# Part of a gate projection moved ahead of the transposes of the attention weights, and ScalarE's copies of them moved ahead of its gate work

## The chip, the cores and the metric

One Trainium2 chip, one of its cores. The number that counts is the time of one execution of the kernel on the device, in microseconds (us); the median of several runs is taken. Engines are called by their short names: PE is TensorE (matmuls), DVE is VectorE, ACT is ScalarE, POOL is GpSimd, SP is SyncE, which only starts transfers here.

## What is computed

The kernel runs two small two-layer blocks over 256 tokens of width 1024, in f32: a recurrent layer, an attention layer, a mixing layer with a convolution, and two feed-forward layers. Only the attention layer is touched:

```python
q, g = jnp.split(h @ w_in, 2, axis=-1)     # 8 heads of 128
s = q @ k.T * sm_scale, causal             # per head, 256 x 256
o = softmax(s) @ v
y = (o * jax.nn.silu(g)) @ w_out
```

With 256 tokens there is one block of keys, so every token attends to itself and the tokens before it.

## The kernel before, in words

**Matmuls.** A weight matrix comes in slabs of 128 x 2048 f32 (1 MB). ACT copies a slab into a rounded high part (line 624, `stream`), DVE subtracts to get the low part (line 1067, shown as L1017, its helper), and PE multiplies three times for each tile: high by high, high by low, low by high (`product`, lines 1578 to 1580). So a gate output, which is one tile of 128 features by 256 tokens summed over 8 input tiles, is 24 matmuls (`gate`, line 1776). `fill(k)` on ACT and on DVE splits all slabs up to k + 3. The raw slabs lie in five buffers, and SP starts a transfer into one as soon as DVE has made the low part of the slab that was in it. Slab 12 + n feeds the gate outputs 2n and 2n + 1.

**Order.** Each engine has its own instruction list, written out by hand, and runs it strictly in order; semaphores tie them together. An output in PSUM goes to one of 8 banks by a fixed table (`outputs`, line 166), and `bank_free` (line 1572) makes PE wait until the bank's last content has been read. Along the way of this stage these are: the output of gate 2 in the bank of the scores of head 0, the transposed weights of head 3 in the bank of gate 0, gate 3 in that of gate 1, and in the second half the transposed weights of head 7 in the bank of gate 4, gate 7 in that of gate 5. The output projection's first two outputs take the banks of gate 6 and of the product of head 4.

**The attention stage** runs twice, for heads 0 to 3 and 4 to 7 (`for h in (0, 4)`):
- PE (lines 1785 to 1794): scores of four heads (L1752, L1753), gate h, gate h+1, the transposes of the weights of heads h and h+1 (`turn_weights`, L1763, three each), gate h+2, the products with the values for h and h+1 (`weighted`, L1772 and L1773), the transposes of h+2 and h+3, gate h+3, the products of h+2 and h+3. After the second half comes the output projection (`block_of("ao", ...)`).
- DVE (lines 1340 to 1354): per head scale and mask (shown as L1020), maxima, negation, inverse of the sum, and the scaling of the weights (L1312, L1313), staggered over the four heads; then a slab's low part, `output` (product times gate), `output_low`, another slab and so on.
- ACT (lines 812 to 824): the exponentials of four heads (L794, L795), the silu of gates h and h+1 (L716), the copies of the transposed weights of h and h+1 from PSUM to SBUF (`turned_weights`, two copies a head), a slab's high part (`fill`), silu of h+2, the high parts of outputs h and h+1 (`output_high`), the copies for h+2 and h+3, silu of h+3, a slab in the first half, and the high parts of h+2 and h+3.

Exp and Silu need different function tables; the load is an instruction of its own on ACT (ACT_TABLE_LOAD). Copies of ACT made through the helper `copy` all carry line 624, and all two-operand instructions of DVE made through `tt_` or `stt` carry 1017 or 1020, so these are told apart by tile and shape: `w<-raw` is a slab, `t<-pb` the turned weights, `r<-t` an output's high or low part. The tiles are f (scores' inputs, silu outputs), acc and s (weights), t (turned weights, outputs), r (high and low parts).

Of the kernel before, what the change touches and what calls it, by code (L numbers as in the profile page):

```python
# [6 lines left out]
P, T, D, KT = 128, 256, 1024, 8  # L7
# [317 lines left out]
def two_block_program(nc, w_d, vec_d, c_d, cst_d, dft_d, rcnt_d, row_d, x_d, out_d):  # L325
# [6 lines left out]
    with ctx:  # L332
        def sb(name, shape, dt=f32):
            return ctx.enter_context(nc.sbuf_tensor(name, shape, dt))

        def sem(name):
            return ctx.enter_context(nc.semaphore(name))
# [8 lines left out]
        R2 = sb("r2", [P, RT, 2, T], f32r)  # L346
# [40 lines left out]
        s_ps = sem("s_ps")  # L387
# [75 lines left out]
        def H(kt):  # L463
            return H0[:, kt, :]

        def out_of(*name):
            return PB[OUT.bank[name]][:, 0:T]

        def bank_of(*name):
            return PB[OUT.bank[name]]  # L470
# [20 lines left out]
        def hi_of(R, i):  # L491
            return R[:, i, 0, :]
# [4 lines left out]
        def ended(*name):  # L497
            return s_ps, OUT.count[name]
# [120 lines left out]
        def _(e):  # L619
# [3 lines left out]
            def copy(out, in_, **kw):  # L623
                return e.activation(out, in_, ACT.Copy, **kw)  # L624
# [14 lines left out]
            def fill(k):  # L639
                stream(MATS[min(k + LOOK, len(MATS) - 1)])  # L640
# [68 lines left out]
            for q in range(2):  # L709
                half = F0f[:, 4 * q:4 * q + 4, :]  # L710
# [3 lines left out]
            def silu_gate(kind, d, F, done):  # L714
                p.wait_ge(*ended(kind, d))
                e.activation(F[:, d, :], out_of(kind, d), ACT.Silu).then_inc(done, 1)  # L716
# [73 lines left out]
            def softmax(heads):  # L790
                for h in heads:
                    mx, s = st8[:, h, :], Sb[h % 4]
                    p.wait_ge(s_ng, h + 1)
                    e.activation(s[:, 0:128], s[:, 0:128], ACT.Exp, bias=mx[:, 2:3], accum_out=mx[:, 4:5])  # L794
                    e.activation(s[:, 128:384], s[:, 128:384], ACT.Exp, bias=mx[:, 3:4],  # L795
                                 accum_out=mx[:, 5:6]).then_inc(s_ex, 1)

            def turned_weights(*heads):
                for h in heads:
                    m, a, b = PB[OUT.bank["t", h]], tt[2 * (h % 2)], tt[2 * (h % 2) + 1]  # L800
                    p.wait_ge(*ended("t", h))
                    if h >= 2:
                        p.wait_ge(*ended("pv", h - 2))
                    copy(a[:, :], m[:, 0:256])
                    copy(b[:, 0:P], m[:, 256:384]).then_inc(s_pt, 1)

            def output_high(*heads):
                for h in heads:
                    p.wait_ge(s_ot, h + 1)
                    copy(hi_of(R1, h), tt[4 + h % 4][:, :]).then_inc(s_ohi, 1)  # L810

            for h in (0, 4):
                softmax(range(h, h + 4))
                silu_gate("ag", h, F3, s_ag)
                silu_gate("ag", h + 1, F3, s_ag)
                turned_weights(h, h + 1)
                fill(12 + h // 2)
                silu_gate("ag", h + 2, F3, s_ag)
                output_high(h, h + 1)
                turned_weights(h + 2, h + 3)  # L820
                silu_gate("ag", h + 3, F3, s_ag)
                if h == 0:
                    fill(13)
                output_high(h + 2, h + 3)
# [744 lines left out]
        def _(e):  # L1569
            p = Port(e)  # L1570

            def bank_free(*name):
                if OUT.prev[name] is not None:
                    p.wait_ge(*freed(OUT.prev[name]))

            def product(out, a_hi, a_lo, b_hi, b_lo, start, stop):

                e.matmul(out, a_hi, b_hi, start=start, stop=False)  # L1578
                e.matmul(out, a_hi, b_lo, start=False, stop=False)  # L1579
                return e.matmul(out, a_lo, b_hi, start=False, stop=stop)  # L1580

            def weights(k):
                p.wait_ge(s_lo, k + 1)

            def tile_of(k, half, o, R, r, out, start, stop, tok):
                w = W[(k + 2) % NSPL]
                if tok:
                    ts = slice(half * P, half * P + P)
                    return product(out, R[:, r, 0, ts], R[:, r, 1, ts], w[:, 0, o:o + 256], w[:, 1, o:o + 256],
                                   start, stop)  # L1590
                cs = slice(o + half * P, o + half * P + P)
                return product(out, w[:, 0, cs], w[:, 1, cs], R[:, r, 0, :], R[:, r, 1, :], start, stop)
# [43 lines left out]
            def spread(out, col):  # L1636

                return e.matmul(out, col.broadcast_to([P, P]), ident, start=True, stop=True)  # L1638

            def plain(out, slab, o, rhs, start, stop):  # L1640

                return e.matmul(out, slab[:, o:o + P], rhs, start=start, stop=stop)  # L1642
# [4 lines left out]
            for a in range(2):  # L1647
                done = e.matmul(bank_of("n", 0)[:, a:a + 1], tt[0][:, a * P:a * P + P], ones_sb[:, 0:1], start=True,
                                stop=True)
# [4 lines left out]
            for a in range(2):  # L1654
                done = spread(bank_of("nr", 0)[:, a * P:a * P + P], c0[:, a:a + 1])
            done.then_inc(s_ps, 1)

            for kt in range(KT):
# [3 lines left out]
                for d in range(8):  # L1662
                    if kt == 0:
                        bank_free("u", d)
                    done = plain(out_of("u", d), slab, d * P, H(kt), kt == 0, kt == KT - 1)
# [13 lines left out]
            for d in range(8):  # L1679
                for kind, name in (("ga", "rg_w_a"), ("gx", "rg_w_x")):  # L1680
# [3 lines left out]
                    for r in (d // 2 * 2, d // 2 * 2 + 1):  # L1684
                        p.wait_ge(s_conv, 6 * (r // 2) + 4 + r % 2 + 1)
                        done = plain(out_of(kind, d), slab, r * 256 + d % 2 * P, F1[:, r, :], r % 2 == 0, r % 2 == 1)
# [4 lines left out]
            for kt in range(KT):  # L1691
                p.wait_ge(s_yt, kt + 1)
                for d in range(4):
# [4 lines left out]
                    done = plain(out_of("y", d), slab, kt * 256 + d % 2 * P, tt[kt][:, :], kt == 0, kt == KT - 1)  # L1698
                    if kt == KT - 1:
                        done.then_inc(s_ps, 1)  # L1700
            for d in range(4, 8):
# [3 lines left out]
                for kt in range(KT):  # L1705
                    done = plain(out_of("y", d), slab, kt * 256 + d % 2 * P, tt[kt][:, :], kt == 0, kt == KT - 1)
# [18 lines left out]
            for kt in range(KT):  # L1725
                keys(kt, (0, 0, ("k", 0)), (0, 1, ("k", 1)), (1, 0, ("k", 2)), (1, 1, ("k", 3)))
                if kt == 3:
                    bank_free("n", 1)
                    p.wait_ge(s_na, 7)
                    for a in range(2):  # L1730
                        done = e.matmul(bank_of("n", 1)[:, a:a + 1], NA[0][:, a * P:a * P + P], ones_sb[:, 0:1],
                                        start=True, stop=True)
                    done.then_inc(s_ps, 1)
                if kt == 5:
                    bank_free("nr", 1)
                    p.wait_ge(s_rc1, 1)
                    for a in range(2):
                        done = spread(bank_of("nr", 1)[:, a * P:a * P + P], c1[:, a:a + 1])
# [7 lines left out]
            def scores(heads):  # L1746
                for h in heads:
                    bank, q, k = PB[OUT.bank["s", h]], F0f[:, h, :], F1[:, h, :]
                    bank_free("s", h)
                    p.wait_ge(s_q, h + 1)  # L1750
                    p.wait_ge(s_k, h + 1)
                    e.matmul(bank[:, 0:128], q[:, 0:128], k[:, 0:128], start=True, stop=True)  # L1752
                    e.matmul(bank[:, 128:384], q[:, 128:256], k, start=True, stop=True).then_inc(s_ps, 1)  # L1753

            def turn_weights(*heads):
                p.wait_ge(s_cst, 16)
                for h in heads:
                    m = PB[OUT.bank["t", h]]
                    bank_free("t", h)
                    p.wait_ge(s_p, h + 1)  # L1760
                    for j in range(3):
                        js = slice(j * P, j * P + P)
                        done = e.transpose(m[:, js], Sb[h % 4][:, js], ident)  # L1763
                    done.then_inc(s_ps, 1)
# [8 lines left out]
                    e.matmul(PB[OUT.bank["pv", h]][:, 128:256], Vt[:, 1, cs], b[:, 0:P], start=False,  # L1773
                             stop=True).then_inc(s_ps, 1)

            def gate(d):
                k = 12 + d // 2
                weights(k)
                bank_free("ag", d)
                p.wait_ge(s_hqlo, 8)  # L1780
                for kt in range(KT):
                    done = tile_of(k, d % 2, kt * 256, R2, kt, out_of("ag", d), kt == 0, kt == KT - 1, False)
                done.then_inc(s_ps, 1)

            for h in (0, 4):
                scores(range(h, h + 4))
                gate(h)
                gate(h + 1)
                turn_weights(h, h + 1)
                gate(h + 2)  # L1790
                weighted(h, h + 1)
                turn_weights(h + 2, h + 3)
                gate(h + 3)
                weighted(h + 2, h + 3)
# [38 lines left out]
            for h in range(4):  # L1833
                bank_free("f", h)
                out = out_of("f", h)
                for a in range(2):
                    p.wait_ge(s_ac, 2 * h + a + 1)
                    e.matmul(out, AC[:, h, a, 0:P], acc[0][:, a * T:a * T + T], start=a == 0, stop=False)
                    done = e.matmul(out, AC[:, h, a, P:256], acc[0][:, (2 + a) * T:(3 + a) * T], start=False,
                                    stop=a == 1)  # L1840
# [9 lines left out]
            for j in range(31):  # L1850
                p.wait_ge(s_dg, j + 1)
                done = e.matmul(out_of("cv", 3), dg[j % 8], G0[:, 3, j:j + T], start=j == 0, stop=j == 30)  # L1852
# [168 lines left out]
            for a in range(2):  # L2021
                for c in range(2):
# [3 lines left out]
                    for g in (2 * c, 2 * c + 1):  # L2026
                        p.wait_ge(s_pq, 4 + g + 1)
                        for b in range(2):
                            done = e.matmul(bank_of("p", a, c)[:, g % 2 * 256:g % 2 * 256 + 256],
                                            rc[:, b, g, a * P:a * P + P], Q[:, b, g, :], start=b == 0, stop=b == 1)  # L2030
# [94 lines left out]
```

## Time and profile before

| | |
|---|---|
| median of 3 runs | 742.0 us (741.99 to 742.11) |
| profiled execution | 742.27 us |
| its span | 740.5 us |
| granted PE clock | 0.999 of full speed |
| busy PE / DVE / ACT | 715.0 / 502.9 / 396.5 us |
| DMA | 156.65 MB, mean 212 GB/s |

The span is what the hardware profiler saw of one execution, from the first to the last instruction; the execution's own time is 1.77 us longer. Matmuls overlap: one of 256 columns has a duration of 0.28 us in the timeline and the next starts 0.12 us later. So the pace of PE is read from starts. A row's bracket gives the idle time before it and what ended it. The stage that is changed runs from 187 to 227 us.

### The profile page before, as it was taken

How to read it: one execution, taken by the hardware profiler on the slowest of the kernel's cores; microseconds unless marked ns; L12 is line 12 of the kernel's file. 1: busy time of each engine (PE TensorE's matmuls, PEld its weight loads, DVE VectorE, ACT ScalarE, POOL GpSimd, SP SyncE). 2: the span in 40 equal slices, each digit the busy share in tenths (PEclk: the TensorE clock that was granted, in tenths of full speed). 3: DMA queues.
4: the chain of work that ended last, by engine and by line, in shares of the span. 5: the costliest groups of instructions: out<-in, count | busy, mean ns of one | idle time of the engine just before them, and what ended most of it. 6: DMA issues, size and time to landing. Idle time of an engine off the chain costs nothing.

```text
span 740.5 us, 9710 instructions
## 1 busy us (share of the span) xinstructions
PE 715.0 (97%) x3902; PEld 625.0 (84%) x3902; DVE 502.9 (68%) x801; ACT 396.5 (54%) x620; POOL 2.4 (0%) x8
## 2 busy tenths in 40 slices
PE   2999999999999999999999999999999999999996
PEld 1888889999899999888888888888878888888885
DVE  4889996999876879976754454555576544555444
ACT  4156545883874776658734434443666344344423
POOL 0000000000000000000000000000000000000000
PEclk9999999999999999999999999999999999999999
DMA  8999994699835342433755545554336445545201
GB/s 336 419 422 415 421 385 163 250 393 340 316 118 216 116 170 71 182 111 150 271 183 183 208 177 177 207 185 171 114 114 227 171 173 208 187 173 201 81 0 58
DMA packets 23229, 156.65 MB, mean 212 GB/s; under 512 B 2576, under 2 KB 2832, under 8 KB 5264
## 3 DMA queue, kind: packets, MB, share of 16 engines
q1 hardware_dynamic: 22608, 153.41, 55.0%
q0 software_dynamic: 576, 2.62, 0.9%
q8 instruction: 31, 0.51, 0.3%
q14 instruction: 14, 0.11, 0.0%
HBM read 154.97 MB, written 1.05 MB: 211 GB/s over the span
## 4 chain that ended last, share of the span: by engine, by line
PE 86%; DVE 8%; ACT 4%; issue 1%; DMA 1%; SPq 0%; DVEq 0%
PE pb L1578 20%; PE pb L1580 20%; PE pb L1579 20%; PE pb L1642 13%; DVE w L1017 3%; DVE raw L1020 2%; PE pb L1852 2%; PE pb L1963 1%; PE pb L1719 1%; PE pb L1718 1%; PE pb L1720 1%; DMA x<-x_dram 1%; ACT w L624 1%; PE pb L1638 1%; PE pb L1885 1%
## 5 line engine op out<-in xcount | busy, mean ns | idle before, releaser
L1017 DVE TENSOR_TENSOR w<-raw,w 128x2048 fp32r<-128x2048 f32 x97 | 221.3, 2291 | 141.1 <-ACT w L624 141.1
L624 ACT ACTIVATE w<-raw 128x2048 fp32r<-128x2048 f32 x97 | 184.7, 1912 | 135.8 <-PE pb L1580 114.7
L1578 PE MATMUL pb<-w,r 128*128 128x512 f32 (+1 forms) x640 | 244.7, 382 | 0.7 <-DVE r L1020 0.3
L1580 PE MATMUL pb<-w,r 128*128 128x512 f32 (+1 forms) x640 | 241.1, 377 | 0.0
L1579 PE MATMUL pb<-w,r 128*128 128x512 f32 (+1 forms) x640 | 240.7, 376 | 0.0
L1578 PEld LDWEIGHTS pb<-w,r 128*128 128x128 f32 x640 | 120.5, 188 | 23.3 <-issue 2.1
L1580 PEld LDWEIGHTS pb<-w,r 128*128 128x128 f32 x640 | 120.4, 188 | 22.5
L1579 PEld LDWEIGHTS pb<-w,r 128*128 128x128 f32 x640 | 120.6, 188 | 21.0
L1578 PE MATMUL pb<-r,w 128*128 128x256 f32 x288 | 82.5, 287 | 0.4 <-DVE r L1017 0.4
L1579 PE MATMUL pb<-r,w 128*128 128x256 f32 x288 | 81.5, 283 | 0.0
L1580 PE MATMUL pb<-r,w 128*128 128x256 f32 x288 | 81.5, 283 | 0.0
L1020 DVE SCALAR_TENSOR_TENSOR raw<-raw,acc 128x1024 f32<-128x1024 f32 x64 | 75.1, 1220 | 4.1 <-DMA raw<-w_dram 4.1
L1642 PE MATMUL pb<-h,ow 128*128 128x256 f32 x256 | 58.5, 392 | 1.7 <-ACT h L686 1.7
L1642 PEld LDWEIGHTS pb<-h,ow 128*128 128x128 f32 x256 | 50.5, 198 | 9.4 <-issue 1.9
L1578 PEld LDWEIGHTS pb<-r,w 128*128 128x128 f32 x288 | 55.2, 192 | 0.6 <-issue 0.6
L1579 PEld LDWEIGHTS pb<-r,w 128*128 128x128 f32 x288 | 55.2, 192 | 0.1
L1580 PEld LDWEIGHTS pb<-r,w 128*128 128x128 f32 x288 | 55.2, 192 | 0.0
L959 ACT ACTIVATE t<-pb,rn 128x256 f32<-128x256 f32 x44 | 20.7, 476 | 59.6 <-PE pb L1580 59.6
L1020 DVE SCALAR_TENSOR_TENSOR f<-f,vec 128x256 f32<-128x256 f32 x114 | 46.6, 480 | 0.2
L1020 DVE SCALAR_TENSOR_TENSOR t<-pb,rn,t 128x256 f32<-128x256 f32 x44 | 21.1, 483 | 22.8 <-ACT t L959 22.8
L1642 PE MATMUL pb<-t,ow 128*128 128x256 f32 x128 | 27.8, 379 | 0.0
L1642 PEld LDWEIGHTS pb<-t,ow 128*128 128x128 f32 x128 | 24.3, 190 | 3.3
(203 smaller groups left out, 657.2 us busy)
## 6 DMA issues: line engine op xcount, KB each, us to landing
raw<-w_dram SPq DMA_DIRECT2D x129, 1024.0 KB, 4.9
ow<-w_dram SPq DMA_DIRECT2D x8, 1024.0 KB, 14.2
ow<-w_dram SPq DMA_DIRECT2D x8, 512.0 KB, 17.0
oh<-w_dram SPq DMA_DIRECT2D x2, 1024.0 KB, 23.1
x<-x_dram SPq DMA_DIRECT2D x2, 512.0 KB, 6.1
f<-rc_dram POOLq DMA_DIRECT2D x1, 1024.0 KB, 5.1
acc<-row_dram POOLq DMA_DIRECT2D x2, 512.0 KB, 6.8
out_dram<-f SPq DMA_DIRECT2D x4, 256.0 KB, 2.3
```

What stands on the lines that cost most here:

```text
L624: return e.activation(out, in_, ACT.Copy, **kw)
L959: e.activation(tt[(at_ - 1) % 4][:, :], bank_of("gu", layer, i, a)[:, 0:T], ACT.Silu, scale=rn[:, 2 * layer, a:a + 1]).then_inc(s_sgt, 1)
L1017: return e.tensor_tensor(out, a, b, op)
L1020: return e.scalar_tensor_tensor(out, a, s, b, op0, op1, **kw)
L1578: e.matmul(out, a_hi, b_hi, start=start, stop=False)
L1579: e.matmul(out, a_hi, b_lo, start=False, stop=False)
L1580: return e.matmul(out, a_lo, b_hi, start=False, stop=stop)
L1638: return e.matmul(out, col.broadcast_to([P, P]), ident, start=True, stop=True)
L1642: return e.matmul(out, slab[:, o:o + P], rhs, start=start, stop=stop)
L1718: e.matmul(with_shift, w[:, 0, o:o + P], raw_key(kt), start=kt == 0, stop=False)
L1719: e.matmul(with_shift, w[:, 1, o:o + P], raw_key(kt), start=False, stop=False)
L1852: done = e.matmul(out_of("cv", 3), dg[j % 8], G0[:, 3, j:j + T], start=j == 0, stop=j == 30)
```

## The change

On PE, the first four of the eight input tiles of gate h+2 (12 matmuls) stand ahead of the transposes of heads h and h+1, and the last four where the whole gate stood; the bank is waited for ahead of the first part, and the semaphore raised at the end of the last. On ACT, `turned_weights(h, h + 1)` comes right after the exponentials, ahead of two silus, and `turned_weights(h + 2, h + 3)` ahead of `output_high(h, h + 1)`. DVE, SP and POOL keep their lists, and the bank table stays.

```diff
@@ scalar
             for h in (0, 4):
                 softmax(range(h, h + 4))
+                turned_weights(h, h + 1)
                 silu_gate("ag", h, F3, s_ag)
                 silu_gate("ag", h + 1, F3, s_ag)
-                turned_weights(h, h + 1)
                 fill(12 + h // 2)
                 silu_gate("ag", h + 2, F3, s_ag)
+                turned_weights(h + 2, h + 3)
                 output_high(h, h + 1)
-                turned_weights(h + 2, h + 3)
                 silu_gate("ag", h + 3, F3, s_ag)
@@ tensor
-            def gate(d):
-                k = 12 + d // 2
+            def gate(d, kts=range(KT)):
+                k, half = 12 + d // 2, d % 2
                 weights(k)
-                bank_free("ag", d)
+                if kts[0] == 0:
+                    bank_free("ag", d)
                 p.wait_ge(s_hqlo, 8)
-                for kt in range(KT):
-                    done = tile_of(k, d % 2, kt * 256, R2, kt, out_of("ag", d), kt == 0, kt == KT - 1, False)
-                done.then_inc(s_ps, 1)
+                for kt in kts:
+                    done = tile_of(k, half, kt * 256, R2, kt, out_of("ag", d), kt == 0, kt == KT - 1, False)
+                if kts[-1] == KT - 1:
+                    done.then_inc(s_ps, 1)
 
             for h in (0, 4):
                 scores(range(h, h + 4))
                 gate(h)
                 gate(h + 1)
+                gate(h + 2, range(0, 4))
                 turn_weights(h, h + 1)
-                gate(h + 2)
+                gate(h + 2, range(4, 8))
                 weighted(h, h + 1)
```

## Rows read from the trace of the kernel before

**Rows 1.** The page, section 1: busy time, share of the span, instructions

```profile
PE 715.0 (97%) x3902; PEld 625.0 (84%) x3902; DVE 502.9 (68%) x801; ACT 396.5 (54%) x620; POOL 2.4 (0%) x8
```

**Rows 2.** Waits of PE, whole span: us in total, times, longest

```profile
PE pb L1772 <- ACT t L624: 1.8, 2, 0.9
...
PE pb L1885 <- DVE x L1017: 0.9, 2, 0.7
```

**Rows 3.** PE's timeline, heads 0 to 3: start, duration, instruction, idle before

```profile
195.24 0.28 PE L1580 MATMUL pb<-r,w 128*128 128x256 f32 x1
195.75 0.52 PE L1763 MATMUL pb<-cst,acc 128*128 128x128 f32 x3 [0.23 <-DVE acc L1313]
197.03 0.52 PE L1763 MATMUL pb<-cst,acc 128*128 128x128 f32 x3 [0.77 <-DVE acc L1313]
197.31 0.36 PE L1578 MATMUL pb<-r,w 128*128 128x256 f32 x1
...
201.24 0.67 PE L1772 MATMUL pb<-t,f 128*128 128x256 f32 x2 [0.82 <-ACT t L624]
...
203.19 0.36 PE L1578 MATMUL pb<-r,w 128*128 128x256 f32 x1
...
206.15 0.60 PE L1772 MATMUL pb<-t,f 128*128 128x256 f32 x2
```

**Rows 4.** PE's timeline, heads 4 to 7

```profile
209.90 0.47 PE L1578 MATMUL pb<-r,w 128*128 128x256 f32 x1
...
215.84 0.82 PE L1763 MATMUL pb<-cst,acc 128*128 128x128 f32 x6
216.41 0.36 PE L1578 MATMUL pb<-r,w 128*128 128x256 f32 x1
...
219.59 0.67 PE L1772 MATMUL pb<-t,f 128*128 128x256 f32 x2
...
221.54 0.36 PE L1578 MATMUL pb<-r,w 128*128 128x256 f32 x1
...
225.61 0.70 PE L1772 MATMUL pb<-t,f 128*128 128x256 f32 x2 [0.95 <-ACT t L624]
...
226.94 0.36 PE L1578 MATMUL pb<-r,w 128*128 128x256 f32 x1
```

**Rows 5.** ScalarE's timeline, 198 to 225 us

```profile
198.69 1.28 ACT L716 ACT_TABLE_LOAD   x1
199.99 0.66 ACT L716 ACTIVATE f<-pb 128x256 f32<-128x256 f32 x2
200.53 1.01 ACT L624 ACTIVATE t<-pb 128x256 f32<-128x256 f32 x4
201.38 1.95 ACT L624 ACTIVATE w<-raw 128x2048 fp32r<-128x2048 f32 x1
...
203.44 0.77 ACT L624 ACTIVATE r<-t 128x256 fp32r<-128x256 f32 x2
...
217.05 1.28 ACT L716 ACT_TABLE_LOAD   x1
...
224.37 0.75 ACT L624 ACTIVATE r<-t 128x256 fp32r<-128x256 f32 x2 [2.41 <-DVE t L1017]
```

**Rows 6.** VectorE's timeline, 203 to 226 us

```profile
203.94 0.76 DVE L1017 TENSOR_TENSOR r<-t,r 128x256 fp32r<-128x256 f32 x2 [0.70 <-ACT r L624]
204.62 2.29 DVE L1017 TENSOR_TENSOR w<-raw,w 128x2048 fp32r<-128x2048 f32 x1
...
209.55 1.01 DVE L1020 SCALAR_TENSOR_TENSOR acc<-pb,cst 128x384 f32<-128x384 f32 x2
...
223.92 0.75 DVE L1017 TENSOR_TENSOR t<-pb,f 128x256 f32<-128x256 f32 x2
224.82 0.76 DVE L1017 TENSOR_TENSOR r<-t,r 128x256 fp32r<-128x256 f32 x2 [0.15 <-ACT r L624]
```

**Rows 7.** ScalarE's timeline, 40 to 46 us

```profile
44.44 0.39 ACT L624 ACTIVATE f<-pb 128x256 f32<-128x256 f32 x1 [0.82 <-PE pb L1642]
```

## The prediction

> **What bounds the kernel now.** The page's busy shares come first: PE is busy 97% of a 740.5 us span [rows 1], so only time in which PE stands still, or a slower PE, is worth anything. The view of PE's waits over the whole span comes second: outside the first stages one group stands out, L1772, the products of attention weights and values, which waited for ScalarE's copies, 1.8 us in two places [rows 2]. The idle times there go by modelled matmul ends, so I priced the stalls from starts in the timeline. Two paces are needed. A whole gate output, 24 matmuls, takes 206.15 - 203.19 = 2.96 us [rows 3], 0.12 each, so half of one is 1.48. Six transposes take 216.41 - 215.84 = 0.57, three 0.29 [rows 4].
>
> Five places where PE stands still between 195 and 227 us:
> - First four heads: gate(1) ends at 195.24 + 0.12 = 195.36, the turn of head 0 starts at 195.75 (0.39 lost).
> - It is through by 196.04; head 1's turn starts at 197.03, released by DVE's scaled weights (0.99 lost).
> - gate(2) runs 197.31 + 2.96 = 200.27; weighted(0) starts at 201.24 (0.97 lost), waiting for ScalarE's copy [rows 3]. ScalarE was in its chain: the table load at 198.69 right behind the exponentials, two silus at 199.99, the copies at 200.53 [rows 5].
> - Second four heads: gate(6) ends at 216.41 + 2.96 = 219.37, weighted(4) starts at 219.59 (0.22 lost). The turns of heads 4 and 5 don't wait.
> - gate(7) ends at 221.54 + 2.96 = 224.50, weighted(6) starts at 225.61 (1.11 lost) [rows 4]. The copies it wants stand on ScalarE behind two high parts, which waited 2.41 us for DVE [rows 5].
>
> Together 3.68 us. That is all this stage can give.
>
> **The change part by part, first half (heads 0 to 3).** Nothing is added or removed: the same matmuls, copies, silus and one table load per half in another order. No DMA moves; the slab copies keep their place among ScalarE's items, save that output_high now follows two turned_weights.
>
> PE puts 12 matmuls of gate(2) ahead of the turns: 195.36 + 1.48 = 196.84. They need slab 13 (gate(2) and gate(3) share it; its low part is well ahead of the softmax on DVE) and the bank of scores 0, which DVE has read by then. Turn 0 has been free to run since 195.75, so it takes 196.84 to 197.13; turn 1's release at 197.03 is past, so it ends at 197.41, 0.10 behind the old 197.31. The other half ends at 197.41 + 1.48 = 198.89. The half gate thus covers both first waits.
>
> ScalarE starts the copies where the table load stood, 198.69. Four copies take a slot of 201.38 - 200.53 = 0.85; from the first copy to weighted(0) it is 201.24 - 200.53 = 0.71 [rows 3, 5]. So weighted(0) starts at 199.40 and 0.51 of waiting is left. Both weighted take (203.19 - 201.24) - 0.57 = 1.38, to 200.78. Next late: head 3's turn writes the bank that silu(0) frees, and the silus are now behind the copies. Load at 199.54, silu at + 1.30 = 200.84 (the 1.30 is 199.99 - 198.69); one silu takes 0.39 (a pair lasts 0.66 and its slot is 0.54, so the second starts 0.27 behind the first), a signal 0.13 (0.71, less the 0.58 that two copies last: 1.01 for four, less half of their slot). Turn 3 is released at 201.36. Turn 2 fills 200.78 to 201.07; 0.29 is waited, and turn 3 ends at 201.65. gate(3) wants the bank of gate(1), freed at 201.11 + 0.39 + 0.13 = 201.63: no wait. gate(3) starts at 201.65, not 203.19: **1.54 us ahead**. It ends at 204.61.
>
> ScalarE: the four items ahead of the slab copy at 201.38 only swap places, so that copy and silu(2) keep their times and ScalarE is free at 203.44 as before [rows 5]. turned_weights(2,3) now stands there: head 2's weights reach PE at 203.44 + 0.71 = 204.15, before gate(3) ends. weighted(2,3) and four scores take 209.90 - 206.15 = 3.75 [rows 3, 4], so gate(4) starts at 208.36, not 209.90.
>
> The price lies on DVE. output_high(0,1) starts 0.85 later, at 204.29, so DVE's output_low starts at 204.79 instead of 203.94, and the slab subtraction queued behind it at 205.47 instead of 204.62 [rows 6], to 207.76 by its 2.29. Then output(2,3), high, low: undisturbed this takes 224.82 + 0.76 - 223.92 = 1.66, to 209.42. The softmax of heads 4 to 7 began at 209.55; before, output_high(2,3) waited for a slab copy on ScalarE, which now starts earlier because silu(3) does. So the delay is hidden and softmax gains 0.13.
>
> **Second half.** gate(4), gate(5): 208.36 + 5.94 (215.84 - 209.90) = 214.30; half of gate(6) to 215.78, turns (ready before) to 216.35, other half to 217.83. ScalarE leaves the exponentials at 217.05 - 0.13 = 216.92; weights reach PE at 217.63: weighted(4) doesn't wait and ends at 219.21. Load at 217.77, silu(4) at 219.07, turn 7's bank at 219.59; turn 6 ends at 219.50, 0.09 is waited, gate(7) starts at 219.88, not 221.54, and ends at 222.84. ScalarE's slab copy starts at 219.61; copy and silu take 203.44 - 201.38 = 2.06, so turned_weights(6,7) starts at 221.67 and head 6's weights are there at 222.38: the 1.11 us wait is gone, since the copies are now ahead of the high parts that wait for DVE. weighted(6,7) takes 226.94 - 225.61 = 1.33, so the output projection starts at **224.17, not 226.94: 2.77 us**. Its second bank is freed by DVE's output(4), the first of a pair that takes 0.75, at about 223.79 + 0.42 + 0.13 = 224.34, wanted three matmuls after the first, 224.17 + 0.37 = 224.54: close, but in time. As a check, stalls left are 0.51 + 0.29 + 0.09 = 0.89, with 3.68 before: 2.79.
>
> **Does it reach the end?** Behind 227 us PE's longest wait is the 0.7 us of L1885 [rows 2], DMA is far from full, and transfers start when a slab has been split, so all moves with PE. I carry 2.77 on, rounded to 2.8. The profiled execution took 742.27 (its span and 1.77 around it), 0.27 over the median of 742.0. 742.27 - 2.8 = 739.5 by the profile, 739.2 against the median.
>
> **A rule against the sum.** By the rows the silu follows 1.30 us after its load is issued, and the load directly follows the exponentials. The Trainium skill (ScalarE: Activation LUTs, What ACT_TABLE_LOAD costs) gives 1283 ns and a drain of about 1380 ns for every switch. The trace agrees with the first figure and shows no drain. What that would make of the time is rival E.
>
> **Rivals.** (A) The copies bring a table load of their own, since they now stand behind Exp. Then two switches of 1.30 each follow the exponentials. First half: weighted(0) at 200.70, turn 3 at 202.66, gate(3) at 202.95 (0.24 ahead), DVE's softmax one load later (about 210.7). Second half: exponentials end near 218.2, weighted(4) at 220.2, gate(7) at 222.5, projection at 226.75, 0.19 ahead: 741.8, no change. Against it: the copy at 44.44 ran behind the Exp of line 690, and what ended its idle time was PE, with no load between [rows 7]. The Trainium skill says the same (ScalarE: Activation LUTs, Table sets: the hidden batching unit): copy is in every set.
>
> (B) DVE's queue eats part of the gain. output_low(0,1), the slab subtraction, output(2,3) and softmax(4) stand behind output_high(0,1). If softmax starts 1.3 us late (210.7), all of ScalarE's times of the second half move with it: gate(7) starts 1.3 later than forecast and half the gain stays: 740.5. For it: the wait chain is real and its slack in the second half is nil once turn 7 waits for silu(4). Against: the 0.85 is known and absorbed.
>
> (C) Slower: the same queue, from the point at which softmax(4) starts over 2.8 us later than forecast, past 212.2. That takes more than one slab subtraction (2.29) of further delay, for instance two in a row (4.58): 4.58 - 2.8 = 1.8 slower, 743.8. Nothing in the rows adds a second one.
>
> (D) The turns are not what PE waits for once the half gate is there, but the half gate costs as much: re-entering the open bank of gate(2) is not seen in the trace. Bounds: nothing (same number of changes between kinds of matmul), or 0.3 us a half (near the 0.39 lost at the first turn, the largest step between kinds that the rows show). I take nothing; upper end 0.6, 739.8.
>
> (E) The silu's table switch, now between the copies and the banks that PE wants, takes longer than 1.30. Each extra us delays the release of turn 3, then softmax(4) with ScalarE's chain, and in the second half turn 7 once more: two us at the projection for each. At 2.77 / 2 = 1.4 extra the gain is gone: 742.0. Against it: the one switch whose follower had nothing else to wait for took 1.30 [rows 5]. The drain that the Trainium skill states in the section above is that case.
>
> **Numbers.** Forecast 0.85 (with D's cost inside), B 0.07, A 0.03, E 0.02, C 0.03. Downward, all five stalls gone would be 3.7: 738.3. The range goes from 738.3 to 740.5, which takes in D and B. A measurement tells 0.2%, 1.5 us, from no change: faster is below 740.5. The forecast and about half of B fall there: 0.88; the other half of B, A and E are the same: 0.09; slower 0.03.
>
> **What the changed profile should show.** PE: twelve matmuls at 195.4 to 196.8, turns with no idle before them, weighted(0) at about 199.4, gate(3) at 201.65 after 0.3 of waiting, scores of heads 4 to 7 about 1.5 earlier, the projection at 224.2. ScalarE: copies at 198.7 and the silu's load at 199.5, and no load ahead of the copies. DVE: slab subtraction at 205.5, softmax(4) at 209.4. It would be wrong if weighted(0) waits past 200, if softmax(4) starts after 210, or if the 2.8 us that PE is ahead at 224 are given back further on.

## The result and the profile after

The changed kernel took 739.29 us, the median of 6 runs (738.29 to 739.67), against 742.0 for the kernel before (740.69 to 742.52): a ratio of 0.9966 with a 95% interval of 0.9955 to 0.9976, 2.7 us faster. In two later sets on other occasions it was 0.9958 (0.9944 to 0.9972) and 0.9952 (0.9939 to 0.9964). The forecast was 739.2. The profiled execution took 739.67, its span 737.9.

The waits of PE over the whole span (total, times, longest; answers to [rows 2]):

```profile
PE pb L1888 <- DVE x L1017: 0.9, 2, 0.7
...
PE pb L1578 <- ACT f L624: 0.4, 1, 0.4
...
PE pb L1772 <- ACT t L624: 0.3, 1, 0.3
PE pb L1763 <- ACT f L716: 0.2, 1, 0.2
```

The wait for the copies has gone from 1.8 to 0.3 us. The small wait at L1763 is the one that the prediction named: turn 3, held by a silu (ACT f L716). PE's timeline through the stage (start, duration, instruction; answers to [rows 3, 4]):

```profile
189.90 0.35 PE L1578 MATMUL pb<-r,w 128*128 128x256 f32 x1 [0.36 <-ACT f L624]
...
197.16 0.92 PE L1763 MATMUL pb<-cst,acc 128*128 128x128 f32 x6
197.83 0.36 PE L1578 MATMUL pb<-r,w 128*128 128x256 f32 x1
...
199.77 0.67 PE L1772 MATMUL pb<-t,f 128*128 128x256 f32 x2 [0.26 <-ACT t L624]
...
201.82 0.55 PE L1763 MATMUL pb<-cst,s 128*128 128x128 f32 x3 [0.17 <-ACT f L716]
202.12 0.36 PE L1578 MATMUL pb<-r,w 128*128 128x256 f32 x1
```

```profile
216.20 0.82 PE L1763 MATMUL pb<-cst,acc 128*128 128x128 f32 x6
216.78 0.36 PE L1578 MATMUL pb<-r,w 128*128 128x256 f32 x1
...
218.28 0.60 PE L1772 MATMUL pb<-t,f 128*128 128x256 f32 x2
...
223.13 0.60 PE L1772 MATMUL pb<-t,f 128*128 128x256 f32 x2
...
224.36 0.36 PE L1578 MATMUL pb<-r,w 128*128 128x256 f32 x1
```

This execution reached gate(0) at 189.90, 0.48 later than the profiled one of before, after a wait of 0.36 that lies outside the change. Its row names ScalarE's copies of two earlier outputs (f), the first of which empties the bank that gate(0) writes; they stood behind the copy of a slab that had landed late:

```profile
187.57 1.91 ACT L624 ACTIVATE w<-raw 128x2048 fp32r<-128x2048 f32 x1 [0.57 <-DMA raw<-w_dram]
...
189.39 0.64 ACT L624 ACTIVATE f<-pb 128x256 f32<-128x256 f32 x2
```

So positions are compared with gate(0): the turns of heads 0 and 1 have no idle time before them, where there were two waits; weighted(0) has 0.26 instead of 0.82; the last weighted, at 223.13, has none. From gate(0) to the output projection PE took 224.36 - 189.90 = 34.46 us; before it was 226.94 - 189.42 = 37.52.

ScalarE behind the exponentials (answers to [rows 5]):

```profile
199.11 0.96 ACT L624 ACTIVATE t<-pb 128x256 f32<-128x256 f32 x4
200.09 1.28 ACT L716 ACT_TABLE_LOAD   x1
201.38 0.66 ACT L716 ACTIVATE f<-pb 128x256 f32<-128x256 f32 x2
...
203.99 1.02 ACT L624 ACTIVATE t<-pb 128x256 f32<-128x256 f32 x4
204.83 0.77 ACT L624 ACTIVATE r<-t 128x256 fp32r<-128x256 f32 x2
```

The copies run right behind the exponentials with no table load ahead of them, the second pair (203.99) is ahead of the high parts (204.83), and the silus 1.29 us after their load begins. VectorE (answers to [rows 6]):

```profile
205.33 0.76 DVE L1017 TENSOR_TENSOR r<-t,r 128x256 fp32r<-128x256 f32 x2 [2.48 <-ACT r L624]
206.01 2.29 DVE L1017 TENSOR_TENSOR w<-raw,w 128x2048 fp32r<-128x2048 f32 x1
...
209.79 1.01 DVE L1020 SCALAR_TENSOR_TENSOR acc<-pb,cst 128x384 f32<-128x384 f32 x2
```

Output_low came late, as forecast, after 2.48 us of waiting, and the slab behind it at 206.01, 16.11 behind gate(0) where it was 15.20 (204.62 [rows 6] - 189.42), but softmax(4) starts at 209.79, which is 19.89 behind gate(0), against 20.13 before (209.55 - 189.42). In the two later traces of the changed kernel it is 19.86 and 19.84.

### The profile page after: what moved, and what is told of

Its sections match the earlier page's. It is cut to its first block, busy times and chain, and to the rows that moved or that the text cites. A ratio compares the mean times of both kernels' runs of the same rounds, so it can differ in the third digit from the quotient of the medians.

```text
span 737.9 us, 9710 instructions
## 1 busy us (share of the span) xinstructions
PE 714.1 (97%) x3902; PEld 624.4 (85%) x3902; DVE 502.4 (68%) x801; ACT 396.3 (54%) x620; POOL 2.4 (0%) x8
## 4 chain that ended last, share of the span: by engine, by line
PE 88%; DVE 6%; ACT 3%; DMA 2%; issue 1%; SPq 0%; DVEq 0%
PE pb L1578 21%; PE pb L1580 21%; PE pb L1579 21%; PE pb L1642 13%; DVE w L1017 2%; PE pb L1855 2%; PE pb L1966 1%; DVE raw L1020 1%; DMA raw<-w_dram 1%; PE pb L1719 1%; PE pb L1718 1%; PE pb L1720 1%; DMA x<-x_dram 1%; PE pb L1888 1%; PE pb L1638 1%
```

## The experiments

All times are medians, with the kernel before run beside them on the same chip; the ratio is worked out from the single executions, so it differs a little from that of the two medians. A time of one execution carries what happened ahead of the stage, so for each trace I also give PE's time from the first matmul of gate(0) to the first of the output projection ("stage"), and within it up to gate(4) ("first half"). They repeat well: the changed kernel gave 34.46, 34.42 and 34.41.

| kernel | time | ratio to before (95%) | stage | first half | second half |
|---|---|---|---|---|---|
| before | 741.5 to 742.0 | 1 | 37.52 | 20.48 | 17.04 |
| changed (after) | 739.29 | 0.9966 (0.9955 to 0.9976) | 34.46 | 18.92 | 15.54 |
| e1, half gate alone | 742.70 | 1.0013 (1.0005 to 1.0022) | 39.15 | 22.10 | 17.05 |
| e2, ScalarE's order alone | 739.46 | 0.9973 (0.9965 to 0.9981) | 34.99 | 19.43 | 15.56 |
| e3, first copies alone | 740.33 | 0.9987 (0.9978 to 0.9995) | 36.45 | 19.41 | 17.04 |
| e4, second copies alone | 740.71 | 0.9985 (0.9976 to 0.9994) | 36.31 | 20.47 | 15.84 |
| after2 | 738.46 | 0.9958 (0.9944 to 0.9972) | 34.42 | 18.89 | 15.53 |
| e5, extra table switch | 741.42 | 1.0000 (0.9992 to 1.0009) | 37.43 | 20.38 | 17.05 |
| e6, half gate and filler | 741.82 | 1.0004 (0.9995 to 1.0013) | 37.47 | 20.41 | 17.06 |
| b3, banks, turn, DVE | 737.27 | 0.9942 (0.9928 to 0.9957) | 33.84 | 18.30 | 15.54 |
| after3 | 738.03 | 0.9952 (0.9939 to 0.9964) | 34.41 | 18.88 | 15.53 |
| b1, banks | 738.53 | 0.9959 (0.9946 to 0.9971) | 34.11 | 18.58 | 15.53 |
| b2, banks and turn | 738.62 | 0.9958 (0.9945 to 0.9972) | 34.13 | 18.57 | 15.56 |
| b3_again | 737.57 | 0.9946 (0.9933 to 0.9958) | 33.85 | 18.31 | 15.54 |

**The parts of the change.** e1 keeps the diff's PE part and puts ScalarE's list back; e2 is the reverse. e3 and e4 move one pair of copies each, with the old PE order:

```diff
 e3
                 softmax(range(h, h + 4))
+                turned_weights(h, h + 1)
                 silu_gate("ag", h, F3, s_ag)
                 silu_gate("ag", h + 1, F3, s_ag)
-                turned_weights(h, h + 1)
 e4
+                turned_weights(h + 2, h + 3)
                 output_high(h, h + 1)
-                turned_weights(h + 2, h + 3)
```

Expected of e1: 

> PE's half of the change alone, ScalarE in its old order. Theory L (a covered wait only moves to the next thing that is late, ScalarE's chain of exponentials, table load, silus, copies): PE is done with gate 2 at 198.9 instead of 200.3 and waits 2.3 us for the copies at weighted(0), which starts at 201.24 as before; the second half has no wait at its turns to cover. No change: 742.0, within 0.3. Rival R (the two waits at the turns, 0.39 + 0.99, are gained outright): 740.6.

Expected of e2: 

> ScalarE's half of the change alone, PE in its old order. Theory L: copies reach PE at 199.4, gate 2 ends at 200.27, so weighted(0) starts then: 0.97 ahead; second half: weighted(4) without its 0.22, weighted(6) without its 1.11. Sum 2.3, time 739.7; the whole change is then only 0.5 better than this part. Rival R (each half of the change removes its own waits): 742.0 less 0.97 + 0.22 + 1.11 is the same 2.3 here, but with the half gate alone at 1.4 the two would have to add to 3.7, which the whole change (2.7) does not show.

Expected of e3: 

> Only turned_weights(h, h+1) moved ahead of the two silus; output_high stays ahead of turned_weights(h+2, h+3), PE old. Theory L: first half 0.97 ahead; in the second half the 0.22 at weighted(4) goes, but the copies for weighted(6) still stand behind the high parts that wait for DVE's slab and output(4), so that wait grows to about 1.4. Sum about 0.9, time 741.1. Rival: that wait stays at 1.11 and 1.2 are gained, 740.8; the trace tells these apart by the idle time ahead of the last weighted.

Expected of e4: 

> Only turned_weights(h+2, h+3) moved ahead of output_high(h, h+1), PE old. Theory L: nothing in the first half (weighted(2) doesn't wait), output_low 0.6 to 0.9 later on DVE but softmax(4) not later; in the second half the wait of 1.11 ahead of weighted(6) goes. Sum 1.1, time 740.9. Rival D (DVE's queue behind output_low eats it): softmax(4) starts later than 209.55 by up to 0.85 and the gain is 0.3, 741.7.

The half gate alone gained nothing, so the waits that it covers are not gained outright. But it also lost about 1 us, which neither theory had. PE's timeline of e1:

```profile
200.50 0.67 PE L1772 MATMUL pb<-t,f 128*128 128x256 f32 x2 [2.27 <-ACT t L624]
...
202.10 1.49 PE L1763 MATMUL pb<-cst,s 128*128 128x128 f32 x6
203.24 0.56 PE L1578 MATMUL pb<-r,w 128*128 128x256 f32 x1
...
204.02 0.41 PE L1578 MATMUL pb<-r,w 128*128 128x256 f32 x1
204.24 0.41 PE L1579 MATMUL pb<-r,w 128*128 128x256 f32 x1
...
205.20 0.28 PE L1578 MATMUL pb<-r,w 128*128 128x256 f32 x1
205.32 0.28 PE L1579 MATMUL pb<-r,w 128*128 128x256 f32 x1
...
207.00 0.60 PE L1772 MATMUL pb<-t,f 128*128 128x256 f32 x2
```

The waits at the turns are one wait now, 2.27 us ahead of weighted(0). In gate(3), from 203.24, one matmul follows the other after about 0.21 us (204.02, 204.24) until about 205.1, and then after 0.12. gate(3) takes 3.76 us instead of 2.96, and the six transposes 1.14 instead of 0.57. The windows of the same trace (start and end, length, then busy time and count of PE, PEld, DVE, ACT and POOL, the granted clock as a share of 2.4 GHz, DMA share and GB/s) say why:

```profile
198.00:200.00 2.00, 0.24 (x3) 0.03 (x1) 1.97 (x4) 1.99 (x4) 0.00 (x0) 1.00 0.16 66
200.00:201.00 1.00, 0.50 (x2) 0.49 (x3) 0.92 (x1) 1.00 (x5) 0.00 (x0) 1.00 0.00 0
201.00:202.00 1.00, 1.00 (x7) 0.93 (x6) 0.42 (x1) 1.00 (x1) 0.00 (x0) 0.82 0.12 33
202.00:203.00 1.00, 1.00 (x7) 1.00 (x7) 0.42 (x1) 1.00 (x3) 0.00 (x0) 0.50 0.43 131
...
205.00:206.00 1.00, 1.00 (x10) 1.00 (x9) 1.00 (x1) 0.00 (x0) 0.00 (x0) 0.97 0.08 33
```

PE was busy for 0.24 of the two us from 198, and from somewhere in 201 to 202 until about 205 the granted clock was 0.50, the lower of its two levels, 1.2 GHz. In the kernel before the same stretch shows 1.00 throughout. e6 tests it.

ScalarE's order alone had a stage of 34.99, 2.53 less than before (expected 2.3), and a median 2.1 less. Its order does nearly all of the work; PE still waits 0.24 and 0.77 at the turns there, but no longer at any weighted. e3 shows how a wait moves when only one is taken away:

```profile
216.75 0.60 PE L1772 MATMUL pb<-t,f 128*128 128x256 f32 x2
...
222.98 0.70 PE L1772 MATMUL pb<-t,f 128*128 128x256 f32 x2 [1.24 <-ACT t L624]
```

The first half is 1.07 shorter, weighted(4) at 216.75 no longer waits, and the wait ahead of weighted(6) has grown from 0.95 [rows 4] to 1.24 (by starts from 1.11 to 1.39, where 1.4 was expected): the second half takes 17.04 us, just as before. e4 is the complement: first half unchanged, 20.47, second half 1.20 shorter. Its rival (DVE's queue eats the gain) fell with it: softmax(4) started 20.12 behind gate(0), as in the kernel before. In the stage e3's 1.07 and e4's 1.21 add to 2.28, and both together make 2.53, since with both the 0.22 at weighted(4) isn't given back at weighted(6).

**Is it the clock?** e6 is e1 with filler work in PE's wait. The transposes go to the bank of product 1, which nobody reads then, and add no result:

```diff
                 gate(h + 2, range(4, 8))
+                if h == 0:
+                    bank_free("pv", 1)
+                    for _ in range(16):
+                        e.transpose(PB[OUT.bank["pv", 1]][:, 0:P], ident, ident)
                 weighted(h, h + 1)
```

Expected of e6: 

> The half gate alone (ScalarE in its old order) with 16 transposes of the identity, written to a bank that nobody reads then, in the wait ahead of weighted(0). They add no result. Theory C (the half gate alone lost 1 us because the 2.27 us of waiting, now in one piece, was followed by 3.4 us at a granted clock of 0.5): the filler takes 1.5 us of the wait, weighted(0) starts when it did, the clock stays at 1.0 and the time is that of the kernel before, within 0.3. Rival T (the loss comes from the split accumulation or from ScalarE's chain): still 1 us slower than before, and gate(3) still takes 3.8 us.

The filler is L1797 in its timeline:

```profile
198.35 1.91 PE L1797 MATMUL pb<-cst 128*128 128x128 f32 x16
200.60 0.70 PE L1772 MATMUL pb<-t,f 128*128 128x256 f32 x2 [0.35 <-ACT t L624]
...
202.59 0.36 PE L1578 MATMUL pb<-r,w 128*128 128x256 f32 x1
...
205.54 0.60 PE L1772 MATMUL pb<-t,f 128*128 128x256 f32 x2
```

```profile
200.00:202.00 2.00, 1.65 (x11) 1.31 (x10) 1.54 (x2) 2.00 (x6) 0.00 (x0) 1.00 0.00 0
202.00:204.00 2.00, 2.00 (x20) 2.00 (x19) 1.03 (x3) 2.00 (x7) 0.00 (x0) 1.00 0.97 254
```

With 0.35 us of wait left the clock stays at 1.00, gate(3) takes 2.95, the first half 20.41 (22.10 in e1) and the time is that of the kernel before. So e1's loss is the clock's: e6 keeps the split gate and ScalarE's old order, and the loss is gone. The executions of e1 say the same. Six of its eleven, the traced one among them, have a mean granted clock of 0.995 and took 742.80 us on average; four have 0.999 and took 741.93, about what e6 took. In e6 all eleven have 0.998 or 0.999.

e6 can't price the split accumulation (the prediction's case D), since PE waits for the copies at weighted(0) and would wait so much less. The second halves of the changed kernel and of e2 can, because neither has a wait between gate(4) and weighted(4): with the split 218.28 - 208.82 = 9.46 us, without it 216.85 - 207.35 = 9.50 (e2's trace). Re-entering the open bank costs nothing.

**Is the silu's switch on the path twice?** e5 puts a third table between the copies and the silus:

```diff
                 turned_weights(h, h + 1)
+                e.activation(k2[:, :], V("eps", 0, 2), ACT.Sqrt)
                 silu_gate("ag", h, F3, s_ag)
```

Expected of e5: 

> The changed kernel with a square root of two numbers between the first copies and the silus, in both halves: one more table load (1.28) and 0.2 of work, about 1.5 us later silus. By rival E of the prediction each us of it costs two at the output projection: +3.0 over the changed kernel, no better than before. Rival: the second half has its own slack and only one of the two counts: +1.5.

```profile
197.59 0.97 ACT L624 ACTIVATE t<-pb 128x256 f32<-128x256 f32 x4
198.57 1.28 ACT L815 ACT_TABLE_LOAD   x1
199.87 0.20 ACT L815 ACTIVATE k<-vec 128x2 f32<-128x2 f32 x1
200.08 1.28 ACT L716 ACT_TABLE_LOAD   x1
201.37 0.66 ACT L716 ACTIVATE f<-pb 128x256 f32<-128x256 f32 x2
```

```profile
201.81 0.55 PE L1764 MATMUL pb<-cst,s 128*128 128x128 f32 x3 [1.68 <-ACT f L716]
...
221.38 0.55 PE L1764 MATMUL pb<-cst,s 128*128 128x128 f32 x3 [1.30 <-ACT f L716]
```

Silus start at 201.37, 1.50 later than without the detour (199.87). The waits ahead of turns 3 and 7 (each the last three transposes before a gate) are 1.68 and 1.30, where they were 0.17 and nothing. The stage is 37.43, 3.01 over that of after2, 1.49 in the first half and 1.52 in the second, and the time 2.96 over. Both halves count in full. The rows also answer the rule that spoke against the sum: a switch takes 1.29 to 1.30 us from its load to the work behind it, twice here (198.57 to 199.87, 200.08 to 201.37). The drain that the Trainium skill adds (ScalarE: Activation LUTs, What ACT_TABLE_LOAD costs) does not show.

**Taking the rest away.** b1 gives turned weights h+3 and gate h+3 the banks of turned weights h and h+1, and the last two products those of gates h and h+1; the second half mirrors it, so that each name finds a bank that was freed early. b2 adds the turn of head h+2 ahead of `weighted(h, h + 1)`. b3 adds one swap on ScalarE and two on DVE:

```diff
 b1: bank table, first half: ag0 6, ag1 7, t0 0, t1 1, ag2 2, pv0 3, pv1 4, t2 5,
-    t3 6, ag3 7, pv2 0, pv3 1
+    t3 0, ag3 1, pv2 6, pv3 7     (second half: 6, 7 and 0, 1 exchanged)
 b2
+                turn_weights(h + 2)
                 weighted(h, h + 1)
-                turn_weights(h + 2, h + 3)
+                turn_weights(h + 3)
 b3, scalar
-                silu_gate("ag", h + 2, F3, s_ag)
                 turned_weights(h + 2, h + 3)
+                silu_gate("ag", h + 2, F3, s_ag)
 b3, vector
             output(0, 1)
+            fill(12)
             output_low(0, 1)
-            fill(12)
...
             fill(13)
-            fill(14)
             output(4, 5)
+            fill(14)
```

Expected of b3: 

> The changed kernel, with the waits that it has left taken away: head 3's turned weights and gate 3 go to the banks of turned weights 0 and 1 (free after the first copies) instead of those of gates 0 and 1 (free after the silus), the turn of head h+2 stands ahead of weighted(h, h+1), turned_weights(h+2, h+3) ahead of silu(h+2), and DVE subtracts its slab ahead of output_low(0, 1) and after output(4, 5). Theory L: 0.2 of wait left at weighted(0), none at turn 3 and none in the second half; 0.6 to 0.7 us under the changed kernel, and softmax(4) about 1.2 us earlier on DVE. Rival: the releases that move are not the ones PE waits for, or ScalarE's copies become late at weighted(2): same as the changed kernel.

Expected of b1: 

> The changed kernel with the new banks alone: turned weights h+3 and gate h+3 in the banks of turned weights h and h+1. Theory L: the 0.3 us of wait at turn 3 goes, little in the second half, where turn 7 no longer waits; gate(0) to the output projection 34.1 us instead of 34.4, 0.3 under the changed kernel. Rival: weighted(2) waits for its copies instead, since gate(3) then ends before they are there; nothing gained.

Expected of b2: 

> The new banks, and the turn of head h+2 ahead of weighted(h, h+1). Theory L: the wait at weighted(0) shrinks by the 0.3 of three transposes, but ScalarE's copies for weighted(2), which stay behind silu(2), are then up to 0.3 late; 0.3 to 0.5 under the changed kernel, 33.9 to 34.1 us of PE's time.

Expected of b3_again: 

> The best version again: 33.84 us from gate(0) to the output projection, 0.6 under the changed kernel, with softmax(4) over 1 us earlier than in the changed kernel.

b1's stage is 34.11 and b2's 34.13: in b1 the wait at turn 3 is gone, in b2 that at weighted(0) too, but then head 2's copies are late:

```profile
203.88 0.67 PE L1777 MATMUL pb<-t,f 128*128 128x256 f32 x2 [0.25 <-ACT t L629]
```

Their times miss what was expected of them: beside after3 (738.03, 737.55 to 738.52) they are 738.53 and 738.62, 0.5 and 0.6 above it and not 0.3 or more below. Their traces took 0.2 us longer behind the stage (513.7 from the output projection to the end, against 513.5); what takes it, and the rest of the difference, stays open. So the 0.3 is shown in the stage and not in the time. b3 removes both waits from the list. Its waits of PE no longer name L1768 or L1777, the turns and products in its numbering; all that are left lie outside the stage, as these two do, at the start and in a later stage:

```profile
PE pb L1653 <- DVE t L1022: 12.5, 1, 12.5
...
PE pb L1894 <- DVE x L1022: 0.9, 2, 0.7
```

Its stage of 33.84 is 37.52 - 3.68, all that the prediction's five places could give. To the hundredth that is chance: gate(3) to weighted(2) is 202.94 - 199.85 = 3.09 where a gate takes 2.96, so some 0.13 of wait is left, and small terms give as much back. softmax(4) starts 1.1 us earlier than in the changed kernel (18.75 behind gate(0)), as expected, but the second half is no shorter for it, 15.54. Of b3's swaps, the one on ScalarE is then what helps by the rows (the copies for weighted(2) start 13.79 behind gate(0), 14.05 in b2); the two kinds were not tried apart. Its time is 1.2 us under the changed kernel in one set (737.27 and 738.46) and 0.5 in the other (737.57 and 738.03). It was the fastest both times; its interval overlaps that of the changed kernel in each set.

## Why the prediction was right, step by step

- **What can be gained.** 3.68 us in five places: b3 gave 37.52 - 33.84 = 3.68.
- **The half gate covers both first waits.** Right: in the changed kernel the turns of heads 0 and 1 follow gate(2)'s first part with nothing between. What the prediction didn't price is the half gate alone; e1 shows that it has worth only with the copies moved: 0.53 us of the stage (34.99 - 34.46).
- **weighted(0), turn 3, gate(3).** Forecast waits 0.51 and 0.29. By starts, measured in after2, the last matmul of gate(2) starts at 198.43, so it ends at 198.55, and weighted(0) starts at 198.90 (0.35); turn 3 is at 200.95 behind a turn 2 at 200.29 + 0.29 (0.37). gate(3), forecast 12.23 behind gate(0), came at 12.22 (after) and 12.18 (after2). That it fits so well is luck in part, since two misses cancel: weighted(0) came 9.87 behind gate(0) in after, where 9.98 was forecast, and the four copies hold ScalarE for 0.98 until the table load (199.11 to 200.09), where 0.85 was taken from a row in which other work follows them.
- **DVE's delay is absorbed.** Forecast 0.13 earlier for softmax(4); 0.24 in after, 0.27 and 0.29 in the later traces. Right in kind, and rival B did not happen.
- **Second half.** No wait at weighted(4), the 1.11 at weighted(6) gone, both right. The 0.09 at turn 7 did not show. Length of the second half: forecast 224.17 - 208.36 = 15.81, measured 15.54.
- **The sum.** The stage was forecast at 224.17 - 189.42 = 34.75 and came to 34.46, so the gain in it is 3.06, where 2.77 was forecast. The 0.29 are small terms, nearly all in the second half. Both pairs of products were priced with the late start of a waiting one: weighted(4,5) at 1.38, where they take 219.59 - 218.28 = 1.31, and weighted(6,7) at 1.33, where they take 224.36 - 223.13 = 1.23. The turns of heads 6 and 7 take 220.18 - 219.59 = 0.59, where 0.57 and 0.09 of waiting were taken. The earlier softmax gives PE nothing, since weighted(4) waits for nothing.
- **To the end.** Right: from the output projection to the end of the span all kernels but b1 and b2 took 513.5 to 513.6 us.
- **Against the times.** The median fell by 2.7 in the first set, the sets after by 3.4 and 3.6. That the first matched 2.8 so closely is in part luck: the stage gained 3.1.
- **Rivals.** A (a load ahead of the copies) is refuted by the row at 199.11. D's price is nothing, as above. E has the right sensitivity, two for one, as e5 shows, but its condition, a longer switch, did not hold. C's delay didn't arise. What none of them had is the clock: half of this edit, without the other half, makes the kernel slower through it.

## What to carry to other kernels

Where several waits follow each other on the engine that bounds, follow the slowest chain behind them: covering an early wait only lengthens the next one until that chain is shortened, and here the chain was the order of copies on an engine that was idle almost half of the time. Put what the bounding engine waits for ahead of what only frees buffers later, and then look at which buffers those are: a bank that is freed by an early step can take the place of one freed by a late step. Before waits are gathered into one, look at the granted clock.

## What the runs showed that was not expected

- **A wait of 2.27 us costs more than itself.** In e1 the granted clock fell to 0.50 about 1 us after PE had gone back to work and stayed there for some 3.4 us; the first half became 1.62 us longer than before. The waits of about 1 us in the kernel before, and the 1.68 of e5, were not followed by a lower clock: 64 executions of the one beside the experiments and 11 of the other all have a mean granted clock of 0.998 or 0.999. The median of e1 rose by 1.2 (the ratio says 1.0) and not by 1.6, and in four of its eleven executions the clock shows no fall. Six of the eleven executions of e3 have 0.997 and took 740.74 us on average, four have 0.999 and took 739.96, and e1, e2 and e4 have one with 0.997 each. No trace of such an execution was kept, so where the clock was lower in it, and whether e3's longer wait (1.24) has to do with it, is open.
- **The executions differ ahead of the stage, not in it.** gate(0) started between 187.86 and 189.90 us in the fourteen traces, while the stage repeats to 0.05 and the rest to 0.3. ScalarE waits there for slabs to land: 9.31 us in the trace of the changed kernel, with the copy at 185.09, and 7.84, with the copy at 182.36, in that of e2. What makes a slab land later was not tried.
